# Rounding fp32 weight tiles on ScalarE straight from the load ring, with VectorE subtracting the rounded tile

## The chip, the cores and the metric

The kernel runs on one core of a Trainium2 chip. The metric is the device time of one launch in microseconds (us), the median of three runs. Engines: TensorE (PE) does matrix products, VectorE (DVE) and ScalarE (ACT) elementwise work, GpSimd (POOL) and SyncE (SP) start transfers.

## The reference

Two layers of an encoder trunk on 512 tokens of width 1024, in fp32. Each layer mixes tokens with 16 heads of three kinds (dilated windows, latent attention, two-dimensional neighbourhood), adds the result, and then mixes channels: layer 0 with a dense SwiGLU, layer 1 with a top-2-of-8 expert SwiGLU. The change touches only the dense one:

```python
def swiglu(h, w1, w3, w2):
    return (jax.nn.silu(h @ w1) * (h @ w3)) @ w2
# h: 512 x 1024 (RMS-normed rows), w1, w3: 1024 x 2816, w2: 2816 x 1024
```

## The kernel before

One program, with a hand-written instruction stream for each engine, in program order; engines meet only through semaphores. The dense channel mixer works in two parts each of an fp32 value, kept in the type fp32r: a high part with the low 12 mantissa bits gone, and a low part, the value minus the high part. A product is then three products: low times high, high times low, high times high.

**Gate/up stage** (line 790): 44 jobs. Job j = 2f is the gate, j = 2f + 1 the up projection of feature tile f (0 to 21, 128 features each). A job is 24 matmuls of 128x512: 8 slices of the model width, 3 products each. It takes weight tile w(j), 128x1024, in three buffers of two parts each (`w5`, WS = 3), and the activations x(0) to x(3) (`xh3` high, `xl3` low). The result goes through SiLU (ScalarE, line 1128) and a product (VectorE, line 1460) to the hidden tile h(f), 128x512.

**w2 stage** (line 801): two passes, i = 0 and 1, over output columns 0 to 511 and 512 to 1023. Step f of a pass takes h(f) and weight tile v(i * 22 + f), 128x512, in three buffers of two parts (`v_parts`, VS = 3), for 4 row tiles with 3 products each: 12 matmuls. The last three f of the second pass are done together once the last tile has its parts.

**Who makes the parts.** `low_part(kind, j)` is a piece of VectorE's stream and `high_part(kind, j)` one of ScalarE's. Both follow one list, SPLITS: w0, w1, x0, w2, x1, x2, x3, w3 to w43, h0, v0, v1, then h1, v2, h2, v3, ... h21, v22, then v23 to v43. In `low_part` VectorE masks the value's bits into one of two scratch tiles `high` (line 1346) and subtracts the scratch tile from the value into the low part (line 1353). In `high_part` ScalarE casts the scratch tile into the high part (line 1057). For x and h tiles the high part lies where the value was, so ScalarE also waits for the subtract (line 1051). A part's buffer must be free first (`parts_free`, waited for by the cast and by the subtract, after the mask). TensorE waits for both parts (`parts_made`). Two semaphores are kept in the order of the list, `low_made` and `high_made`; a third, `masked`, counts masks.

**Around the entry.** In layer 0, for each row tile t from 0 to 3, VectorE's order is: add the attention output to x (line 1318), low part of w(t) for t < 3, reciprocal and scaled row (lines 1201 and 1213), then, for row tile t - 1, copy of its transposed half (line 1188) and low part of x(t-1). ScalarE's is: square sum and root of t (lines 985 and 992), high part of w(t), then copy and high part of x(t-1). TensorE runs the output projection of t and transposes the rows of t - 1.

**The ring.** Weights come through `weight_ring`, two halves. An entry is two loads of 1 MB (w1 and w3, four w tiles) or one of 2.8 MB (eleven v tiles). SyncE issues the load of an entry when the low part of the last tile in the entry two before is made (line 461). Nothing in TensorE's or SyncE's stream is changed.

Of the kernel before, what the change touches and what calls it, by code (L numbers as in the profile page):

```python
# [25 lines left out]
ALU = mybir.AluOpType  # L26
# [3 lines left out]
P = 128  # L30
SEQ, D, LAYERS = 512, 1024, 2
# [41 lines left out]
FT = DFF // P  # L73
# [14 lines left out]
WS = 3  # L88
VS = 3
# [65 lines left out]
def split_order():  # L155


    order = [("w", 0), ("w", 1), ("x", 0), ("w", 2), ("x", 1), ("x", 2), ("x", 3)]
    order += [("w", j) for j in range(WS, 2 * FT)] + [("h", 0), ("v", 0), ("v", 1)]
    for f in range(1, FT):  # L160
        order += [("h", f), ("v", f + 1)]
    return order + [("v", n) for n in range(FT + 1, 2 * FT)]


SPLITS = split_order()


def split_of(kind, j):
    return SPLITS.index((kind, j))


class Jobs:
# [27 lines left out]
def trunk(nc, a):  # L200
# [3 lines left out]
    with ctx:  # L204
        def sb(name, cols, dt=F32, rows=P):
            return ctx.enter_context(nc.sbuf_tensor(name, [rows, cols], dt))

        def sem(name):
            return ctx.enter_context(nc.semaphore(name))
# [3 lines left out]
        x = sb("x_rows", NT * D)  # L213
# [64 lines left out]
        xh3, xl3 = (v[:, :].rearrange("p (k s) -> p k s", k=ND) for v in (x_high, x_low))  # L278
# [3 lines left out]
        hh3 = h_high[:, :].rearrange("p (f s) -> p f s", f=FT)  # L282
# [3 lines left out]
        v_parts = [w_parts[:, o:o + 2 * SEQ].rearrange("p (j c) -> p j c", j=2) for o in (4 * D, 5 * D, 3 * D)]  # L286
        w5 = w_parts[:, :].rearrange("p (b j k c) -> p b j k c", b=WS, j=2, k=ND)
        at = (FT + 22) * SEQ
        high = A0[:, at:at + 2 * D].rearrange("p (b k c) -> p b k c", b=2, k=ND)
# [61 lines left out]
        loaded = [sem("ring_loaded_0"), sem("ring_loaded_1")]  # L351
# [20 lines left out]
        masked, low_made, high_made = sem("bits_masked"), sem("low_parts_made"), sem("high_parts_made")  # L372
# [23 lines left out]
        for l in range(LAYERS):  # L396
# [10 lines left out]
            if l == 0:  # L407
                w1, w3, w2 = a["w1"][0], a["w3"][0], a["w2"][0]
# [9 lines left out]
        n_of = {e[0]: n for n, e in enumerate(entries)}  # L418
        loads_to = [0, 0]
        full_at = []  # L420
# [4 lines left out]
        def wview(key, i=0):  # L425
            n = n_of[key]
            o, k, c, _ = entries[n][1][i]
            s = (n % 2) * RING + o
            return ring[:, s:s + k * c].rearrange("p (k c) -> p k c", k=k)
# [6 lines left out]
        NG = 7  # L436

        block = ctx.enter_context(nc.Block())

        def parts_free(engine, kind, j):  # L440

            if kind == "w" and j >= WS:
                engine.wait_ge(filled, J.filled(0, "gu"[(j - WS) % 2], (j - WS) // 2))
            elif kind == "v" and j < VS:
                engine.wait_ge(filled, J.filled(0, "u", FT - 2 if j < 2 else FT - 1))
            elif kind == "v" and j - VS == FT - 1:
                engine.wait_ge(filled, J.filled(0, "d", 0, NT - 1))
            elif kind == "v":
                engine.wait_ge(w2_used, j - VS + 1 - (j - VS >= FT))

        @block.sync
        def _(sp):
# [4 lines left out]
            for n, (key, loads, last) in enumerate(entries):  # L457
                if n >= 2:
                    last_use = entries[n - 2][2]
                    if last_use[0] == "split":  # L460
                        sp.wait_ge(low_made, split_of(*last_use[1:]) + 1)
                    else:
                        sp.wait_ge(filled, J.filled(*last_use))
                for (o, k, c, src) in loads:
                    s = (n % 2) * RING + o
                    sp.dma_start(ring[:, s:s + k * c].rearrange("p (k c) -> p k c", k=k), src)\
                        .then_inc(loaded[n % 2], 16)
                if n == 0:
                    for t in range(2, NT):
                        sp.dma_start(x3[:, t, :], a["x"][0, t * P:(t + 1) * P, :]).then_inc(x_in[t], 16)  # L470
                    sp.dma_start(tab[:, T_COS:], a["tables"][:, T_COS:]).then_inc(tab_in, 16)
# [131 lines left out]
        def _(pe):  # L603
# [75 lines left out]
            for l in range(LAYERS):  # L679
# [104 lines left out]
                if l == 0:  # L784
                    for j in range(2 * FT):
                        b = take(l, "gu"[j % 2], j // 2)
                        parts_made(max(split_of("w", j), split_of("x", NT - 1)))
                        for k in range(ND):
                            for w, xx in ((1, xh3), (0, xl3), (0, xh3)):
                                last = nc.tensor.matmul(b, w5[:, j % WS, w, k, :], xx[:, k, :],  # L790
                                                        start=(k == 0 and w == 1), stop=(k == ND - 1 and xx is xh3 and w == 0))
                        last.then_inc(filled, 1)
# [169 lines left out]
        def _(act):  # L962
# [76 lines left out]
            def second_norm_turned(l, t):  # L1039
                copy_out(split((l, "h2", t, 0)), (l, "h2", t, 0))  # L1040
                if l == 0:
                    high_part("x", t)

            def high_part(kind, j):

                if (kind, j) not in SPLITS:
                    return
                n = split_of(kind, j)
                act.wait_ge(masked, n + 1)
                if kind in "xh":  # L1050
                    act.wait_ge(low_made, n + 1)
                else:
                    parts_free(act, kind, j)
                dst = {"x": lambda: xh3[:, :, j * P:(j + 1) * P], "w": lambda: w5[:, j % WS, 0, :, :],
                       "h": lambda: hh3[:, j, :], "v": lambda: v_parts[j % VS][:, 0, :]}[kind]()
                src = high[:, n % 2] if kind in "xw" else high[:, n % 2].rearrange("p k c -> p (k c)")[:, 0:SEQ]
                nc.scalar.copy(dst, src).then_inc(high_made, 1)  # L1057

            def expo(l, g):
# [11 lines left out]
            for l in range(LAYERS):  # L1071
# [39 lines left out]
                for t in range(NT):  # L1111
                    act.wait_ge(emptied["D"], J.emptied(l, "op", t, 1))
                    x_root(t, A0[:, NT * D:NT * D + D] if l == 0 else yT[:, ND // 2:, :].rearrange("p k s -> p (k s)"))
                    if l == 0 and t < WS:
                        high_part("w", t)
                    if t:
                        second_norm_turned(l, t - 1)
# [56 lines left out]
        def _(dve):  # L1174
# [145 lines left out]
            def low_part(kind, j):  # L1320

                if (kind, j) not in SPLITS:
                    return
                n = split_of(kind, j)
                f = j // 2
                if kind == "x":
                    dve.wait_ge(emptied["A"], J.emptied(0, "h2", j, 0))
                    dve.wait_ge(emptied["D"], J.emptied(0, "h2", j, 1))
                    src, dst = hT3[:, :, j * P:(j + 1) * P], xl3[:, :, j * P:(j + 1) * P]
                elif kind == "h":  # L1330
                    dve.wait_ge(emptied["D"], J.emptied(0, "u", j))
                    src, dst = hid[:, j, :], hl3[j]
                else:
                    if kind == "w":
                        e, v = n_of[(0, "f", f // 2)], wview((0, "f", f // 2), j % 2)
                        src, dst = v[:, :, (f % 2) * P:(f % 2) * P + P], w5[:, j % WS, 1, :, :]
                    else:
                        i, k = divmod(j, FT)
                        c, k = divmod(k, FT // 2)
                        e, src, dst = n_of[(0, "w2", i, c)], wview((0, "w2", i, c))[:, k, :], v_parts[j % VS][:, 1, :]  # L1340
                    dve.wait_ge(loaded[e % 2], full_at[e])
                top_part = high[:, n % 2] if kind in "xw" else high[:, n % 2].rearrange("p k c -> p (k c)")[:, 0:SEQ]
                if n >= 2:
                    dve.wait_ge(high_made, n - 1)
                    dve.wait_ge(low_made, n - 1)
                nc.vector.tensor_scalar(top_part.bitcast(I32), src.bitcast(I32), HIGH, None, ALU.bitwise_and)\  # L1346
                    .then_inc(masked, 1)
                dve.wait_ge(masked, n + 1)
                if kind == "h" and j:
                    dve.wait_ge(filled, J.filled(0, "u", FT - 1))  # L1350
                else:
                    parts_free(dve, kind, j)
                nc.vector.tensor_tensor(dst, src, top_part, ALU.subtract).then_inc(low_made, 1)

            def attention_added(t):
                add_to_x(l, ("op", t, 1), t, 1)
                if l == 0 and t < WS:
                    low_part("w", t)
# [259 lines left out]
```

## Time and profile before

| | |
|---|---|
| median of 3 runs | 2644.17 us (2642.98 to 2645.36) |
| the profiled execution's own time | 2649.0 us |
| its span, first to last instruction | 2647.1 us |
| granted TensorE clock, mean | 0.970 |
| busy: TensorE, VectorE, ScalarE | 93%, 24%, 19% of the span |
| gate/up stage (line 790) | from 425.26 us |
| w2 stage (line 801) | from 671.87 us |

The busy shares are means over the whole kernel; what a change in one stage does is read from that stage. Of a wait that TensorE has, the row says in brackets how long it was idle and who released it. Matmuls overlap in the records: the distance of two starts, not a duration, is what one costs.

### The profile page before, as it was taken

Reading aid. Unit: us, or ns where it says so; the run is one execution under the profiler, and the core shown is the slowest. Engines: PE = TensorE matmul, PEld = TensorE weight load, DVE = VectorE, ACT = ScalarE, POOL = GpSimd, SP = SyncE. Lnnn points to the kernel's source line nnn. Section 1 sums busy time; section 2 is a strip of 40 time slices with the busy share of each in tenths; the row PEclk is TensorE's granted clock in tenths of the full one; section 3 lists DMA queues with packets and bytes.
Section 4 is the critical chain, followed back from the end, with each engine's and each line's share of the span. In section 5 each row is a group of like instructions: output and inputs, shape, how many; then the busy total and the mean of one; then the engine's idle time right before and its main releaser. Section 6 shows DMA issues by size and latency. Waiting matters only on the chain.

```text
span 2647.1 us, 38548 instructions
## 1 busy us (share of the span) xinstructions
PE 2472.9 (93%) x16160; PEld 2162.3 (82%) x16161; DVE 646.9 (24%) x1382; ACT 507.8 (19%) x1032; POOL 115.9 (4%) x100
## 2 busy tenths in 40 slices
PE   8989998999999899997998999999989999999994
PEld 5658656888886568646998999999989999999994
DVE  2146435333742345522000000010000010101003
ACT  1135323222421235411010001001010010100102
POOL 2011000000001020101000000000000000000001
PEclk9999999999999899998999999999999999999997
DMA  8201164223230200144875665776767767788783
GB/s 251 80 13 35 46 222 123 92 92 105 73 118 28 79 32 15 47 167 150 307 295 207 245 230 222 275 261 262 287 255 259 281 252 295 290 309 298 276 302 112
DMA packets 203139, 482.34 MB, mean 182 GB/s; under 512 B 4833, under 2 KB 31600, under 8 KB 202592
## 3 DMA queue, kind: packets, MB, share of 16 engines
q1 hardware_dynamic: 192208, 429.36, 44.2%
q0 software_dynamic: 8304, 40.82, 4.9%
q10 hardware_dynamic: 2448, 9.44, 0.9%
q8 instruction: 154, 2.52, 0.4%
q14 instruction: 25, 0.20, 0.0%
HBM read 459.93 MB, written 35.39 MB: 187 GB/s over the span
## 4 chain that ended last, share of the span: by engine, by line
PE 77%; issue 3%; DVE 2%; ACT 1%; DMA 0%; POOL 0%; DVEq 0%; ACTq 0%; POOLq 0%
PE ps L891 33%; PE ps L906 16%; PE ps L790 9%; PE ps L632 6%; PE ps L801 4%; PE ps L640 3%; PE ps L746 2%; PE ps L625 1%; PE ps L875 1%; PE ps L847 1%; PE ps L859 1%; DVE k_low L1267 0%; ACT qk_high L1026 0%; DVE x_rows L1560 0%; PE ps L726 0%
## 5 line engine op out<-in xcount | busy, mean ns | idle before, releaser
L891 PE MATMUL ps<-hT,attention_arena 128*128 128x128 f32 (+4 forms) x4096 | 530.2, 288 | 43.7 <-issue 43.7
L891 PEld LDWEIGHTS ps<-hT,attention_arena 128*128 128x128 f32 x4096 | 515.3, 195 | 45.5 <-issue 45.5
L1549 DVE TENSOR_TENSOR attention_arena<-ps,attention_arena 128x256 f32<-128x256 f32 x224 | 95.2, 425 | 1238.1 <-ACT attention_arena L1162 1238.1
L891 PE MATMUL ps<-hT,weight_ring 128*128 128x128 f32 (+4 forms) x3072 | 388.6, 283 | 0.0
L891 PEld LDWEIGHTS ps<-hT,weight_ring 128*128 128x128 f32 x3072 | 376.8, 191 | 0.0
L1162 ACT ACTIVATE attention_arena<-ps 128x256 f32<-128x256 f32 x224 | 85.9, 383 | 1128.7 <-PE ps L891 1128.6
L906 PE MATMUL ps<-attention_arena 128*128 128x128 f32 (+4 forms) x2048 | 266.0, 283 | 0.0
L632 PE MATMUL ps<-weight_ring,hT 128*128 128x384 f32 (+3 forms) x768 | 257.6, 496 | 3.3 <-DVE hT L1188 1.7
L906 PEld LDWEIGHTS ps<-attention_arena 128*128 128x128 f32 x2048 | 254.1, 191 | 0.0
L632 PEld LDWEIGHTS ps<-weight_ring,hT 128*128 128x128 f32 x768 | 146.4, 192 | 105.9 <-issue 61.5
L790 PE MATMUL ps<-x_high,w_parts 128*128 128x512 f32 x704 | 223.0, 398 | 5.6 <-ACT x_high L1057 5.6
L906 PE MATMUL ps<-attention_arena,weight_ring 128*128 128x128 f32 (+4 forms) x1536 | 199.5, 283 | 0.0
L906 PEld LDWEIGHTS ps<-attention_arena,weight_ring 128*128 128x128 f32 x1536 | 190.5, 191 | 0.0
L625 PE MATMUL ps<-tables,attention_arena 128*128 128x128 f32 (+1 forms) x840 | 131.1, 288 | 42.3 <-DVE attention_arena L1213 15.6
L625 PEld LDWEIGHTS ps<-tables,attention_arena 128*128 128x128 f32 (+1 forms) x840 | 107.9, 148 | 72.1 <-issue 29.5
L790 PEld LDWEIGHTS ps<-x_high,w_parts 128*128 128x128 f32 x704 | 132.7, 188 | 36.7 <-issue 5.9
L746 PE MATMUL ps<-attention_arena 128*128 128x128 f32 (+1 forms) x1024 | 140.8, 282 | 2.9 <-ACT attention_arena L1100 2.1
L640 PE MATMUL ps<-hT,weight_ring 128*128 128x512 f32 x320 | 141.2, 595 | 0.0
L790 PE MATMUL ps<-x_low,w_parts 128*128 128x512 f32 x352 | 137.8, 392 | 0.0
L746 PEld LDWEIGHTS ps<-attention_arena 128*128 128x128 f32 x1024 | 128.7, 197 | 7.4 <-ACT attention_arena L1100 3.6
L1057 ACT CAST w_parts<-attention_arena 128x1024 fp32r<-128x1024 f32 (+1 forms) x88 | 73.7, 837 | 226.3 <-DVE attention_arena L1346 107.9
L640 PEld LDWEIGHTS ps<-hT,weight_ring 128*128 128x128 f32 x320 | 60.0, 192 | 69.0 <-issue 68.4
(185 smaller groups left out, 1811.5 us busy)
## 6 DMA issues: line engine op xcount, KB each, us to landing
attention_arena<-in_e_w_dram SPq DMA_DIRECT2D x96, 2048.0 KB, 12.3
weight_ring<-in_e_w_dram SPq DMA_DIRECT2D x72, 2048.0 KB, 12.2
weight_ring<-in_w_dram SPq DMA_DIRECT2D x22, 1024.0 KB, 7.3
weight_ring<-in_w_dram SPq DMA_DIRECT2D x4, 2816.0 KB, 10.0
results_by_slot<-attention_arena ACTq DMA_DIRECT2D x9, 1024.0 KB, 9.8
weight_ring<-in_w_o_dram SPq DMA_DIRECT2D x4, 2048.0 KB, 7.9
attention_arena<-rows_by_slot POOLq DMA_DIRECT2D x8, 1024.0 KB, 11.4
weight_ring<-in_w_in_dram SPq DMA_DIRECT2D x2, 3072.0 KB, 10.6
```

The source lines that it names most:

```text
L625: last = nc.tensor.transpose(b[0:w, i * P:(i + 1) * P], s, ident)
L632: last = nc.tensor.matmul(b[:, 0:n], lhsT[:, k, t * P:(t + 1) * P], w[:, k, c0:c0 + n], start=(k == 0), stop=(k == kt - 1))
L640: last = nc.tensor.matmul(b[:, :], w[:, k, c0:c0 + P], hT3[:, k, :], start=(k == 0), stop=(k == ND - 1))
L746: last = nc.tensor.matmul(ob[:, t * P:t * P + v.shape[1]], pt[:, g % 2, k * P:(k + 1) * P], v, start=(k == 0), stop=(k == NT - 1))
L790: last = nc.tensor.matmul(b, w5[:, j % WS, w, k, :], xx[:, k, :], start=(k == 0 and w == 1), stop=(k == ND - 1 and xx is xh3 and w == 0))
L801: last = nc.tensor.matmul(banks[t], h[:, t * P:(t + 1) * P], v[:, j, :], start=(f == 0 and n == 0), stop=(f == FT - 1 and n == 2))
L847: last = nc.tensor.matmul(ps[:, 6 + i % 2, k * UNIT:(k + 1) * UNIT], h4[:, t, (2 * i + k) * P:(2 * i + k + 1) * P], hot[:, t, :], start=(t ...
L891: last = nc.tensor.matmul(ps[:, f % 2, m * UNIT:m * UNIT + n], w[:, k, i * P:(i + 1) * P], XT[:, k, 0:n], start=(k == 0), stop=(k == ND - 1))
L906: last = nc.tensor.matmul(ps[:, 2 + d // 2, at:at + n], w[:, i, d * P:(d + 1) * P], eh[:, f % EHS, 0:n], start=(f == 0 and d % 2 == 0), st ...
L1057: nc.scalar.copy(dst, src).then_inc(high_made, 1)
L1162: nc.scalar.activation(esil[:, f % 2, :], ps[:, f % 2, 0:UNIT], ACT.Silu).then_inc(e_silu, 1)
L1549: tt(eh[:, f % EHS, :], ps[:, f % 2, UNIT:2 * UNIT], esil[:, f % 2, :], ALU.mult).then_inc(gu_free, 1)
```

## The change

Weight tiles (kinds w and v) are no longer masked. ScalarE waits for the load of the ring entry and for the buffer, and casts the tile from the ring to fp32r, which rounds it; VectorE waits for this cast and subtracts the high part from the tile. For x and h tiles mask, subtract and cast stay as they were; their scratch tile is now chosen by their own count, IN_PLACE, and its reuse waits for the cast of the tile two before in that count.

```diff
+IN_PLACE = [n for n, (kind, j) in enumerate(SPLITS) if kind in "xh"]
...
+        def raw_part(kind, j):
+
+            if kind == "w":
+                f = j // 2
+                return n_of[(0, "f", f // 2)], wview((0, "f", f // 2), j % 2)[:, :, (f % 2) * P:(f % 2) * P + P]
+            i, k = divmod(j, FT)
+            c, k = divmod(k, FT // 2)
+            return n_of[(0, "w2", i, c)], wview((0, "w2", i, c))[:, k, :]
...
                 n = split_of(kind, j)
-                act.wait_ge(masked, n + 1)
                 if kind in "xh":
+                    m = IN_PLACE.index(n)
+                    act.wait_ge(masked, m + 1)
                     act.wait_ge(low_made, n + 1)
+                    dst = xh3[:, :, j * P:(j + 1) * P] if kind == "x" else hh3[:, j, :]
+                    src = high[:, m % 2] if kind == "x" else high[:, m % 2].rearrange("p k c -> p (k c)")[:, 0:SEQ]
                 else:
+                    e, src = raw_part(kind, j)
+                    dst = w5[:, j % WS, 0, :, :] if kind == "w" else v_parts[j % VS][:, 0, :]
+                    act.wait_ge(loaded[e % 2], full_at[e])
                     parts_free(act, kind, j)
...
                 nc.scalar.copy(dst, src).then_inc(high_made, 1)
...
                 n = split_of(kind, j)
-                f = j // 2
+                if kind in "wv":
+                    _, src = raw_part(kind, j)
+                    dst = w5[:, j % WS, 1, :, :] if kind == "w" else v_parts[j % VS][:, 1, :]
+                    top_part = w5[:, j % WS, 0, :, :] if kind == "w" else v_parts[j % VS][:, 0, :]
+                    dve.wait_ge(high_made, n + 1)
+                    nc.vector.tensor_tensor(dst, src, top_part, ALU.subtract).then_inc(low_made, 1)
+                    return
...
-                if n >= 2:
-                    dve.wait_ge(high_made, n - 1)
-                    dve.wait_ge(low_made, n - 1)
+                m = IN_PLACE.index(n)
+                top_part = high[:, m % 2] if kind == "x" else high[:, m % 2].rearrange("p k c -> p (k c)")[:, 0:SEQ]
+                if m >= 2:
+                    dve.wait_ge(high_made, IN_PLACE[m - 2] + 1)
                 nc.vector.tensor_scalar(top_part.bitcast(I32), src.bitcast(I32), HIGH, None, ALU.bitwise_and)\
                     .then_inc(masked, 1)
-                dve.wait_ge(masked, n + 1)
+                dve.wait_ge(masked, m + 1)
```

## Rows read from the trace of the kernel before

**Rows 1.** Busy time by stage: us, then busy us (instructions) of each engine, granted clock, DMA share.

```profile
core 0: us, PE busy (x) PEld busy (x) DVE busy (x) ACT busy (x) POOL busy (x), PEclk, DMA share, GB/s
425.00:672.00 247.00, 246.74 (x1057) 199.39 (x1058) 91.90 (x108) 57.37 (x68) 3.04 (x6) 0.99 0.34 108
672.00:733.00 61.00, 61.00 (x268) 49.78 (x267) 47.22 (x91) 26.38 (x43) 0.00 (x0) 1.00 0.24 86
733.00:794.00 61.00, 60.14 (x263) 49.00 (x262) 24.54 (x48) 16.70 (x28) 0.00 (x0) 1.00 0.27 95
```

**Rows 2.** Line 1346 (mask), weight tiles: count, ns min/median/max, first and last start, shapes.

```profile
L1346 DVE TENSOR_SCALAR attention_arena<-weight_ring x88: 417/552/694, 393.2 to 782.9; 128x1024 int32<-128x1024 int32 x44, 128x512 int32<-128x512 int32 x44
```

**Rows 3.** Timeline, the entry: start us, us, engine, line, what [idle before, releaser].

```profile
399.85 1.23 DVE L1353 TENSOR_TENSOR w_parts<-weight_ring,attention_arena 128x1024 fp32r<-128x1024 f32 x1
...
400.64 1.03 ACT L1057 CAST w_parts<-attention_arena 128x1024 fp32r<-128x1024 f32 x1
...
403.89 1.23 DVE L1353 TENSOR_TENSOR x_low<-hT,attention_arena 128x1024 fp32r<-128x1024 f32 x1
...
406.27 0.69 DVE L1318 TENSOR_TENSOR x_rows<-ps,x_rows 128x512 f32<-128x512 f32 x1 [1.15 <-PE ps L632]
...
407.00 1.06 ACT L985 ACTIVATE attention_arena<-x_rows 128x1024 f32<-128x1024 f32 x1 [0.74 <-DVE x_rows L1318]
...
407.60 1.23 DVE L1353 TENSOR_TENSOR w_parts<-weight_ring,attention_arena 128x1024 fp32r<-128x1024 f32 x1
...
408.38 1.03 ACT L1057 CAST w_parts<-attention_arena 128x1024 fp32r<-128x1024 f32 x1
...
411.63 1.23 DVE L1353 TENSOR_TENSOR x_low<-hT,attention_arena 128x1024 fp32r<-128x1024 f32 x1
...
412.95 1.05 ACT L1057 CAST x_high<-attention_arena 128x1024 fp32r<-128x1024 f32 x1 [3.06 <-DVE x_low L1353]
...
414.01 0.69 DVE L1318 TENSOR_TENSOR x_rows<-ps,x_rows 128x512 f32<-128x512 f32 x1 [1.15 <-PE ps L632]
...
414.74 1.06 ACT L985 ACTIVATE attention_arena<-x_rows 128x1024 f32<-128x1024 f32 x1 [0.74 <-DVE x_rows L1318]
...
415.92 0.29 ACT L992 ACTIVATE small<-small,tables 128x1 f32<-128x1 f32 x1
...
416.25 0.16 DVE L1201 RECIPROCAL small<-small 128x1 f32<-128x1 f32 x1 [1.54 <-ACT small L992]
```

**Rows 4.** Timeline of ScalarE and of VectorE, an attention preparation at 211 us.

```profile
211.11 0.58 ACT L1017 CAST qk_high<-ps 96x512 fp32r<-96x512 f32 x1
...
211.80 0.69 DVE L1254 TENSOR_TENSOR q_low<-ps,qk_high 96x512 fp32r<-96x512 f32 x1 [0.41 <-ACT qk_high L1017]
```

**Rows 5.** Timelines of VectorE, ScalarE and TensorE, first pass over w2.

```profile
672.68 0.42 DVE L1346 TENSOR_SCALAR attention_arena<-attention_arena 128x512 int32<-128x512 int32 x1
673.13 0.69 DVE L1353 TENSOR_TENSOR x_low<-attention_arena 128x512 fp32r<-128x512 f32 x1
673.74 0.42 DVE L1346 TENSOR_SCALAR attention_arena<-weight_ring 128x512 int32<-128x512 int32 x1
...
673.91 0.62 ACT L1057 CAST h_high<-attention_arena 128x512 fp32r<-128x512 f32 x1 [6.82 <-DVE x_low L1353]
674.43 0.62 ACT L1057 CAST w_parts<-attention_arena 128x512 fp32r<-128x512 f32 x1
...
674.67 0.47 PE L801 MATMUL ps<-w_parts,x_low 128*128 128x512 f32 x1
...
732.48 0.39 PE L801 MATMUL ps<-w_parts,h_low 128*128 128x512 f32 x1
```

**Rows 6.** Timeline of TensorE, the first matmuls of the gate/up stage.

```profile
425.26 0.77 PE L790 MATMUL ps<-x_high,w_parts 128*128 128x512 f32 x1 [5.56 <-ACT x_high L1057]
...
428.27 0.39 PE L790 MATMUL ps<-x_low,w_parts 128*128 128x512 f32 x1
```

**Rows 7.** Timelines of VectorE and TensorE, the last tile of w2.

```profile
785.03 0.69 DVE L1353 TENSOR_TENSOR w_parts<-weight_ring,attention_arena 128x512 fp32r<-128x512 f32 x1 [1.69 <-PE ps L801]
...
785.78 0.49 PE L801 MATMUL ps<-w_parts 128*128 128x512 f32 x1 [0.86 <-DVE w_parts L1353]
```

More of the change, by code:

```diff
@@ L1048, in high_part @@
                 n = split_of(kind, j)
-                act.wait_ge(masked, n + 1)
                 if kind in "xh":
+                    m = IN_PLACE.index(n)
+                    act.wait_ge(masked, m + 1)
                     act.wait_ge(low_made, n + 1)
-                else:
+                    dst = xh3[:, :, j * P:(j + 1) * P] if kind == "x" else hh3[:, j, :]
+                    src = high[:, m % 2] if kind == "x" else high[:, m % 2].rearrange("p k c -> p (k c)")[:, 0:SEQ]
+                else:
+                    e, src = raw_part(kind, j)
+                    dst = w5[:, j % WS, 0, :, :] if kind == "w" else v_parts[j % VS][:, 0, :]
+                    act.wait_ge(loaded[e % 2], full_at[e])
                     parts_free(act, kind, j)
-                dst = {"x": lambda: xh3[:, :, j * P:(j + 1) * P], "w": lambda: w5[:, j % WS, 0, :, :],
-                       "h": lambda: hh3[:, j, :], "v": lambda: v_parts[j % VS][:, 0, :]}[kind]()
-                src = high[:, n % 2] if kind in "xw" else high[:, n % 2].rearrange("p k c -> p (k c)")[:, 0:SEQ]
                 nc.scalar.copy(dst, src).then_inc(high_made, 1)
@@ L1329, in low_part @@
                     src, dst = hT3[:, :, j * P:(j + 1) * P], xl3[:, :, j * P:(j + 1) * P]
-                elif kind == "h":
+                else:
                     dve.wait_ge(emptied["D"], J.emptied(0, "u", j))
                     src, dst = hid[:, j, :], hl3[j]
[L1333 to L1342, printed above, removed]
-                if n >= 2:
-                    dve.wait_ge(high_made, n - 1)
-                    dve.wait_ge(low_made, n - 1)
+                m = IN_PLACE.index(n)
+                top_part = high[:, m % 2] if kind == "x" else high[:, m % 2].rearrange("p k c -> p (k c)")[:, 0:SEQ]
+                if m >= 2:
+                    dve.wait_ge(high_made, IN_PLACE[m - 2] + 1)
                 nc.vector.tensor_scalar(top_part.bitcast(I32), src.bitcast(I32), HIGH, None, ALU.bitwise_and)\
                     .then_inc(masked, 1)
-                dve.wait_ge(masked, n + 1)
+                dve.wait_ge(masked, m + 1)
                 if kind == "h" and j:
```

## Prediction

> **What bounds the kernel now.** I read three views in order. The table by stage comes first: in the dense channel mixer (425 to 794 us) TensorE is busy 246.74 of 247, 61.00 of 61 and 60.14 of 61 us, at a granted clock of 0.99 to 1.00, while VectorE is busy 91.9, 47.2 and 24.5 us and ScalarE less [rows 1]. So work taken off VectorE is worth nothing here by itself; what counts is when the parts of a tile are ready. Second, the instructions of the mask line: 88 of the 114 masks are on weight tiles, 44 of 1024 columns (0.69 us) and 44 of 512 (0.42 us), 48.8 us of VectorE in all [rows 2]. Third, the timeline of VectorE and ScalarE at the three places where TensorE does wait, or nearly does, for a part: the entry (399 to 425 us), the steps f = 1 to 21 of the first pass over w2 (674 to 733 us) and the last tile of w2 (785 us). All three are weighed below.
>
> **What the change does to the order.** Before, a weight tile cost VectorE mask then subtract, and ScalarE's cast ran beside the subtract. After, ScalarE casts the tile itself and VectorE's subtract waits for that cast. The mask goes (−0.69 or −0.42 us of VectorE), but cast and subtract, which overlapped, now stand one behind the other. On VectorE the waiting subtract holds up whatever is queued behind it: at the entry the reciprocal and normed row of the same t, in the loop over w2 the mask of the next hidden tile. No DMA is added or moved past another in any queue. SP's load into a half of the ring waits for the subtract of the last tile that lay there; the other half then holds four jobs of work (22 us, below), and a load that is asked for 1 to 6 us later is late by that against TensorE too, whose own steps slip with it: nobody waits.
>
> Where the change costs nothing: in the gate/up stage (44 tiles, 41 of them there) a tile is split when its buffer is released and is read two jobs later. A job is 24 matmuls, 247 us over 44 jobs, 5.6 us [rows 1]; cast plus subtract is 1.03 + 1.23 = 2.3 us [rows 3]. Cover is 11 us, so nothing is gained by the mask that goes nor lost by the order. The same holds for the second pass over w2: 0.62 + 0.69 = 1.3 us against two steps of 2.75 us (below).
>
> **The handoff cast to subtract** is not in the old dense code, but the attention preparation does just this: a cast to fp32r from 211.11 for 0.58 us, and a subtract that reads it, from 211.80, so 0.11 us later; it lasts 0.69 us, as long as the subtract with a masked operand [rows 4, 5]. The nearest other case is a root and the reciprocal that waits for it: ends 416.21, starts 416.25, 0.04 us [rows 3]. Bounds 0.04 and 0.11; I take 0.06: nearer to the reciprocal, because the new subtract, like it, has one wait in front of it, where the one at 211 us waits for a bank of TensorE too.
>
> **Term 1, the entry.** The order on VectorE is: add(t), split of w(t), reciprocal and row(t), copy and split of x(t−1). On ScalarE: square and root(t), cast w(t), copy and cast x(t−1) [rows 3].
> - t = 1: cast w1 starts 400.64, lasts 1.03, handoff 0.06: subtract at 401.73 instead of 399.85, +1.88. That also moves the subtract of x0 from 403.89 to 405.77.
> - An instruction begins a little before the one ahead of it ends: 0.08 us on VectorE (673.13 + 0.69 against 673.74), 0.10 on ScalarE (673.91 + 0.62 against 674.43) [rows 5]. So VectorE is free for add(2) 1.23 − 0.08 = 1.15 us after that subtract's start, at 406.92, where TensorE let it go at 406.27: +0.65. The cast of x0 starts 1.32 us after the subtract of x0 (the distance that 411.63 and 412.95 show for x1), at 407.09; ScalarE is free 1.05 − 0.10 later, at 408.04. So square(2) starts at 408.04 instead of 407.00, +1.04: slack of the old order is used up.
> - t = 2: cast w2 408.38 + 1.04 = 409.42, ends 410.45, subtract at 410.51 instead of 407.60, +2.91. The subtract of x1 goes from 411.63 to 414.54, its cast from 412.95 to 415.86.
> - t = 3: add(3) at 414.54 + 1.15 = 415.69 instead of 414.01; square(3) after the cast of x1, at 415.86 + 0.95 = 416.81 instead of 414.74, **+2.1 us**. From here to the first dense matmul at 425.26 everything is a chain without slack (root, row, turn, copy, split x2, copy, split x3; TensorE waits 5.56 us for the last cast) [rows 6], so 2.1 us stays. Bounds: 0, if the shorter split of w hid it all, which the order excludes, and with 0.11 twice 2.2; the low bound with 0.04 is 2.05.
>
> **Term 2, the first pass over w2.** The splits run h1, v2, h2, v3, ... and each queue is in order. Start to start in the old trace [rows 5]: mask h to subtract h 0.45 (672.68, 673.13); subtract h to cast h 0.78 (673.91), since the cast of a hidden tile overwrites its source and waits; cast h to cast v 0.52 (674.43). New: cast v lasts 0.62, handoff 0.06, subtract v; then 0.61 from a subtract's start to the next mask's (673.13, 673.74). This is a ring, as VectorE waits for cast v and ScalarE for subtract h: 0.45 + 0.78 + 0.52 + 0.62 + 0.06 + 0.61 = 3.04 us for each f. In the old order VectorE's own four instructions bounded the loop at 2 × (0.45 + 0.61) = 2.12 us, shorter than TensorE's step. TensorE's step: f = 1 starts at 674.67 and the second pass at 732.48 [rows 5], 21 steps of 2.75 us. The lead is gone already at f = 1: its cast ends at 674.53, 0.14 us before the start. So every step after it is late by 0.29 us more: 20 × (3.04 − 2.75) = 5.8 us, and about 0.1 us for an exposed weight load at the last wait (at 785.78 the first matmul lasts 0.49 against 0.39 [rows 5, 7]): **+5.9 us**. The buffers don't slow the ring, since with a late TensorE v(f+1) has had its buffer free for a step. Bounds: handoff 0.04 gives 3.02 and 5.5, 0.11 gives 3.09 and 6.9.
>
> The loop puts 20 new gaps of some 0.3 us into a stretch without any. After the 5.56 us idle at the entry 7 matmuls take from 425.26 to 428.27, 0.43 us each, which is the 1.2 GHz level [rows 6]; but the 0.86 us wait at 785 left the granted clock of 733 to 794 us at 1.00 [rows 1, 7], and a new gap is a third of it. I take no fall of the clock; it is a rival. The Trainium skill (TensorE: Matmul & The Clock Gate, Part 1: The HAM clock gate) says that the array's clock is gated down to half when TensorE was too little busy of late, which speaks against a change that thins out a full stretch. By that rule, did it bite here, the sum would be that of the rival "the clock falls" below; by the row it is the sum below.
>
> **Term 3, the last tile.** v43's buffer is free when step f = 18 of the second pass ends. Old: subtract at 785.03, for 0.69, matmul at 785.78. New: the cast starts where the subtract did, lasts 0.62, handoff 0.06, subtract at 785.71: **+0.7 us** [rows 7].
>
> **Sum.** 2.1 + 5.9 + 0.7 = 8.7 us. Behind 794 us nothing of the change runs, and the later stages start from the dense result, so the delay goes through to the end. The profiled execution took 2649.0 us with a span of 2647.1; it would take 2657.7, span 2655.8. The median of the runs was 2644.17, 4.8 us under it; with the same sum 2652.9 us. (0.2%, about what a measurement here can tell, is 5.3 us.)
>
> **Rivals.**
> - *The ring is no ring.* If ScalarE or VectorE got ahead (v cast under the subtract of h, say), the loop would stay at TensorE's 2.75 us; then only 2.1 + 0.7: 2647.0 us. For it: the margin is only 0.29 us of 3.04. Against: the program order of both queues. Deciding point: a ring under 2.75.
> - *A dearer ring.* ScalarE now reads a strided slice of the ring, and VectorE reads an fp32r operand beside an SBUF one; no row has just these. The sequence at 211 us says 0.69 us for the subtract. Were cast or handoff 0.2 us longer, the loop would cost 20 × 0.2 = 4.0 more, entry and end 0.6 more: 2657.5 us.
> - *Not slower: the masks take memory time from TensorE.* In gate/up 1056 matmuls fill 246.6 us (247 us less the 0.3 before the first), 0.2335 each; between 672 and 733 the records give 61.00/268 = 0.2276 [rows 1]. Were the masks the difference, 1056 × 5.9 ns = 6.2 us would come back and 2.5 us stay: 2646.7 us, no change that a measurement tells. Against: gate/up has less VectorE work per us (91.9 of 247) than the stage behind it (47.2 of 61), and is the slower [rows 1]. It decides from 3 ns a matmul (3.4 us back, 5.3 left); above 8 ns the kernel would be faster.
> - *The clock falls in the loop.* At 0.43 us a step is 5.16 us: 20 × (5.16 − 3.04) = 42 us more, 2695 us. The wait of 0.86 us that cost no clock speaks against. (The page named under term 2 has the rule by which this could come.)
> - *The change does nothing:* excluded, since the removed masks and the new wait are certain instructions; what can fail is only that they reach TensorE (first rival).
>
> **How the numbers follow.** Forecast 0.66, own range 2651 to 2655; no ring 0.13; dearer ring 0.11; masks steal 0.06; clock 0.02; faster through something I don't see 0.02. Range 2646.5 to 2657: it takes in forecast and "no ring", and leaves out the upper half of the dearer ring, the clock, and what is faster. Faster: 0.03 (the unseen one, a part of the fourth). Slower: forecast nearly whole (0.61), dearer ring and clock, 0.74. Within 0.2%: 0.23.
>
> **What the profile after would show.** Right: mask rows only on x and hidden tiles (26), the subtract of weight tiles each behind its ScalarE cast; first dense matmul at about 427.4; between 676 and 740 us casts of h_high every 3.04 us, and TensorE idle before about 20 matmuls with the h_high cast as releaser, some 0.2 us each; the second pass begun near 740.5; a wait of 1.5 us at the last tile; granted clock 1.00 throughout. Wrong: cast distance still 2.77; or matmul spacing below 0.2334 us in gate/up; or a first dense matmul before 426.

## The result, and the profile after

| | before | changed |
|---|---|---|
| median, us | 2650.34 (9 runs) | 2660.71 (9 runs) |
| lowest to highest | 2642.98 to 2650.90 | 2652.84 to 2661.51 |
| ratio | | 1.0041, 95% interval 1.0029 to 1.0053 |
| the profiled execution: own time, span | 2649.0, 2647.1 | 2660.71, 2658.7 |

The change makes the kernel slower, by 10.4 us in the medians (7.7 to 14.0 by the interval), where 8.7 was forecast. The time itself lies outside the stated range: the nine runs of the kernel before have a median 6.2 us above that of the three which the sum was put on.

The page of the changed kernel, busy time of each engine. VectorE is 41.8 us less busy than before, and the kernel is slower.

```profile
span 2658.7 us, 38285 instructions
...
PE 2482.0 (93%) x16160; PEld 2163.9 (81%) x16161; DVE 605.1 (23%) x1294; ACT 505.8 (19%) x1032; POOL 116.3 (4%) x100
```

Busy time by stage of the changed kernel, for gate/up, first and second pass over w2 [rows 1]:

```profile
429.00:676.00 247.00, 246.99 (x1055) 199.53 (x1056) 67.06 (x66) 57.02 (x67) 2.79 (x6) 0.99 0.33 108
676.00:742.00 66.00, 65.65 (x265) 47.92 (x265) 38.30 (x67) 24.48 (x43) 0.00 (x0) 1.00 0.17 61
742.00:804.40 62.40, 60.91 (x266) 49.63 (x265) 18.85 (x30) 16.63 (x28) 0.00 (x0) 1.00 0.32 113
```

Gate/up is as long as it was, although VectorE works 67 us in it and not 92. The first pass is longer, and TensorE looks nearly as busy in it as ever (65.65 of 66): the recorded durations of matmuls overlap and so cover a gap of 0.2 us. The gaps show in the starts.

Timeline of the changed kernel, the entry (rows of TensorE, VectorE and ScalarE) [rows 3, 6]:

```profile
400.06 1.04 PE L637 MATMUL ps<-tables,attention_arena 128*128 128x128 f32 x8
...
402.37 1.03 ACT L1072 CAST w_parts<-weight_ring 128x1024 fp32r<-128x1024 f32 x1
...
403.43 1.23 DVE L1345 TENSOR_TENSOR w_parts<-weight_ring,w_parts 128x1024 fp32r<-128x1024 f32 x1 [2.48 <-ACT w_parts L1072]
...
411.12 1.03 ACT L1072 CAST w_parts<-weight_ring 128x1024 fp32r<-128x1024 f32 x1
...
412.19 1.23 DVE L1345 TENSOR_TENSOR w_parts<-weight_ring,w_parts 128x1024 fp32r<-128x1024 f32 x1 [2.88 <-ACT w_parts L1072]
...
418.50 1.05 ACT L997 ACTIVATE attention_arena<-x_rows 128x1024 f32<-128x1024 f32 x1
...
429.01 0.77 PE L802 MATMUL ps<-x_high,w_parts 128*128 128x512 f32 x1 [5.50 <-ACT x_high L1072]
```

The first row is the transposes of row tile 0. The same row of the kernel before, with those at which its first pass over w2 begins and its second ends:

```profile
398.33 1.04 PE L625 MATMUL ps<-tables,attention_arena 128*128 128x128 f32 x8
...
671.87 0.39 PE L801 MATMUL ps<-w_parts,h_low 128*128 128x512 f32 x1
...
794.07 1.03 PE L625 MATMUL ps<-tables,attention_arena 128*128 128x128 f32 x8
```

So the transposes stood at 398.33. All of this stretch is 1.73 us late already when it begins, and that comes from ahead of the changed code. Set against its own beginning, the first dense matmul comes at 28.95 us (429.01 − 400.06), before at 26.93 (425.26 − 398.33). VectorE now waits 2.48 and 2.88 us for the casts of w1 and w2. The square sum of row tile 3 starts at 418.50, 2.03 us later than before on the same clock (414.74 + 1.73).

Timelines of the changed kernel, first pass over w2 [rows 5]:

```profile
677.54 0.69 DVE L1365 TENSOR_TENSOR x_low<-attention_arena 128x512 fp32r<-128x512 f32 x1
679.49 0.69 DVE L1345 TENSOR_TENSOR w_parts<-weight_ring,w_parts 128x512 fp32r<-128x512 f32 x1 [1.26 <-ACT w_parts L1072]
680.10 0.42 DVE L1358 TENSOR_SCALAR attention_arena<-attention_arena 128x512 int32<-128x512 int32 x1
680.56 0.69 DVE L1365 TENSOR_TENSOR x_low<-attention_arena 128x512 fp32r<-128x512 f32 x1
...
678.32 0.62 ACT L1072 CAST h_high<-attention_arena 128x512 fp32r<-128x512 f32 x1 [6.82 <-DVE x_low L1365]
678.85 0.62 ACT L1072 CAST w_parts<-weight_ring 128x512 fp32r<-128x512 f32 x1
681.34 0.62 ACT L1072 CAST h_high<-attention_arena 128x512 fp32r<-128x512 f32 x1 [1.87 <-DVE x_low L1365]
...
676.28 0.40 PE L813 MATMUL ps<-w_parts,h_low 128*128 128x512 f32 x1
...
679.08 0.47 PE L813 MATMUL ps<-w_parts,x_low 128*128 128x512 f32 x1
...
682.10 0.47 PE L813 MATMUL ps<-w_parts,x_low 128*128 128x512 f32 x1
...
742.24 0.39 PE L813 MATMUL ps<-w_parts,h_low 128*128 128x512 f32 x1
```

The ring in these rows: subtract h 677.54, cast h 678.32, cast v 678.85 (ends 679.47), subtract v 679.49, mask h 680.10, subtract h 680.56. One round is 3.02 us. Both helpers are idle in it, VectorE 1.26 and ScalarE 1.87 us, each waiting for the other, and TensorE for both (679.08 to 682.10). The rows of line 813 in the changed kernel name this idle time:

```profile
its engine sat idle before it (us, times) until:
  issue: 8.6, 21
  DVE w_parts L1345: 3.4, 2
```

Twenty-one gaps have no releaser: the profile gives them to "issue", on the weight load, not to the cast of h_high as the prediction had it. The first of them (0.30 us, at 679) stands in the kernel before too (0.28); the other twenty are the change's. What they wait for has to be read from the equal distances: the casts of h_high are 3.02 us apart over the whole pass, and so are TensorE's steps.

Timelines of the changed kernel, the last tile [rows 7]:

```profile
794.77 0.62 ACT L1072 CAST w_parts<-weight_ring 128x512 fp32r<-128x512 f32 x1 [2.10 <-PE ps L813]
...
795.42 0.69 DVE L1345 TENSOR_TENSOR w_parts<-weight_ring,w_parts 128x512 fp32r<-128x512 f32 x1 [2.02 <-ACT w_parts L1072]
...
796.17 0.50 PE L813 MATMUL ps<-w_parts 128*128 128x512 f32 x1 [1.49 <-DVE w_parts L1345]
```

1.49 us idle where it was 0.86.

### The profile page after: what moved, and what is told of

It is laid out like the page before. It is cut to its first block, busy times and chain, and to the rows that moved or that the text cites. A ratio compares the mean times of both kernels' runs of the same rounds, so it can differ in the third digit from the quotient of the medians.

```text
span 2658.7 us, 38285 instructions
## 1 busy us (share of the span) xinstructions
PE 2482.0 (93%) x16160; PEld 2163.9 (81%) x16161; DVE 605.1 (23%) x1294; ACT 505.8 (19%) x1032; POOL 116.3 (4%) x100
## 4 chain that ended last, share of the span: by engine, by line
PE 77%; issue 3%; DVE 2%; ACT 1%; DMA 0%; POOL 0%; DVEq 0%; ACTq 0%; POOLq 0%
PE ps L903 33%; PE ps L918 16%; PE ps L802 9%; PE ps L644 6%; PE ps L813 5%; PE ps L652 3%; PE ps L758 2%; PE ps L637 1%; PE ps L887 1%; PE ps L859 1%; PE ps L871 1%; DVE k_low L1282 0%; ACT qk_high L1038 0%; DVE x_rows L1572 0%; PE ps L738 0%
## 5 line engine op out<-in xcount | busy, mean ns | idle before, releaser
L1345 DVE TENSOR_TENSOR w_parts<-weight_ring,w_parts 128x1024 fp32r<-128x1024 f32 (+1 forms) x88 | 84.2, 958 | 180.5 <-ACT w_parts L1072 180.5
```

## The experiments

The theory (A): the loss is the serial order of cast and subtract at three places, and nothing else of the change costs or saves. Its rivals (B and C in the expectations): the masks disturb TensorE; the direct rounding or the fp32r operand is dear by itself; the change slows something outside the dense stage.

The main evidence is one table of stages, a profile of each kernel. A stage runs between the starts of TensorE instructions: entry, from the transposes of row tile 0 (line 625 before, at 398.33) to the first gate/up matmul; then gate/up, the first pass, and the second pass with its last tile up to the first transposes of layer 1 (at 794.07 before). Outside is the span less these four. us:

| kernel | entry | gate/up | pass 1 | pass 2 | sum | outside | ratio to before, 95% |
|---|---|---|---|---|---|---|---|
| before | 26.9 | 246.6 | 60.6 | 61.6 | 395.7 | 2251.4 | |
| before_again | 26.9 | 247.6 | 60.6 | 61.6 | 396.7 | 2246.5 | one run |
| changed | 29.0 | 247.3 | 66.0 | 62.2 | 404.4 | 2254.3 | 1.0041 (1.0029 to 1.0053) |
| after_again | 29.0 | 246.7 | 65.9 | 62.2 | 403.8 | 2248.0 | 1.0029 (1.0020 to 1.0038) |
| after_third | 29.0 | 247.3 | 66.0 | 62.2 | 404.4 | 2255.1 | one run |
| only_w | 29.0 | 246.6 | 60.6 | 61.6 | 397.8 | 2250.8 | 1.0007 (0.9998 to 1.0015) |
| only_v | 26.9 | 247.6 | 66.0 | 62.2 | 402.7 | 2254.3 | 1.0025 (1.0015 to 1.0034) |
| order_alone | 29.1 | 247.2 | 67.9 | 62.3 | 406.5 | 2254.1 | 1.0052 (1.0039 to 1.0065) |
| order_one_wait | 28.9 | 246.7 | 66.0 | 62.2 | 403.8 | 2247.8 | 1.0044 (1.0031 to 1.0057) |
| mask_first | 29.0 | 247.3 | 60.6 | 62.2 | 399.1 | 2248.1 | 1.0013 (1.0004 to 1.0022) |
| cast_early | 26.9 | 246.6 | 66.0 | 62.2 | 401.7 | 2249.7 | 1.0031 (1.0022 to 1.0040) |
| all_mended | 26.9 | 246.6 | 60.6 | 60.9 | 395.0 | 2250.9 | 1.0002 (0.9993 to 1.0011) |

Entry, pass 1 and pass 2 repeat to 0.1 us from launch to launch. Outside doesn't: 2246.5 to 2255.1. That is why the three stages, and not the whole time, decide below.

**after_again: the changed kernel once more.**

> The changed kernel once more, beside the kernel before on the same chip. Theory A (the serial order of cast and subtract makes the loss at three places; what is left of the difference is the granted clock elsewhere): from the first transposes of the second norm to the first transposes of layer 1 it takes 404.4 us again, against 395.7 before, so 8.7 us more, and the rest of the span differs from the first profile by some us in either direction with the granted clock. Theory B (the change costs time outside the dense stage too): the stretches outside are 3 us longer than before again.

2655.67 us against 2648.03: +7.6. The dense stage takes 403.8 us, as expected by A within the scatter of gate/up; outside it is 3.4 us shorter than in the unchanged kernel's first profile, and 1.5 longer than in its second, where B asked for 3 us longer.

**only_w and only_v: each half of the change.**

```diff
+RAW = "w"
-IN_PLACE = [n for n, (kind, j) in enumerate(SPLITS) if kind in "xh"]
+IN_PLACE = [n for n, (kind, j) in enumerate(SPLITS) if kind not in RAW]
...
-                if kind in "wv":
+                if kind in RAW:
...
```

only_v has "v" there. The other kind of weight tile keeps its mask, its scratch tile and the old waits.

> Only the w tiles (gate/up) are rounded straight from the ring, v tiles are masked as before. Theory A: 2.0 us over before, all of it between the second norm and the first dense matmul; h_high casts about 2.75 us apart. Theory C (44 masks of 0.69 us fewer speed gate/up): gate/up shorter by 3 us or more, so at most as slow as before.

> Only the v tiles (w2) are rounded straight from the ring, w tiles are masked as before. Theory A: 6.0 us over before, 5.4 in the first pass over w2 and 0.6 at the last tile; no change at the entry. Rival: the loop is slow only because TensorE comes to it with another lead after the late entry; then under 3 us.

only_w has the changed kernel's entry and the old kernel's two passes; only_v the reverse. The stage sums are 2.1 and 7.0 us over before; without gate/up, 2.1 and 6.0. In only_w gate/up takes 246.6 us with its masks of weight tiles gone, exactly as in the first profile of before: masks don't disturb TensorE there. That the late entry changes the lead at the loop is out too. In time: 2650.18 (+2.2, with an interval that takes in no change) and 2655.41 (+7.4).

**order_alone: the old masks, the new order.**

```diff
                     parts_free(dve, kind, j)
+                if kind in "wv":
+                    dve.wait_ge(high_made, n + 1)
                 nc.vector.tensor_tensor(dst, src, top_part, ALU.subtract).then_inc(low_made, 1)
```

> The kernel before, masks and scratch tile kept, with one wait added: the subtract of a weight tile waits for ScalarE's cast of it. Theory A (order alone): the masks lie in VectorE's waiting time, so it is as slow as the changed kernel, 8 to 9 us over before; casts of hidden tiles 3.02 us apart in the first pass over w2. Theory B (the direct rounding, a strided source or an fp32r operand, costs its own time): less than 4 us over before. Theory C (the masks disturb TensorE): gate/up is at 0.2335 us a matmul here and faster in the changed kernel.

The order alone gives the whole loss, 10.8 us in the stages, so the loss needs neither the rounding from the ring nor the fp32r operand. But it gives more than the whole: 2662.57 us, +14.5, and a round of the ring of 3.12 us (688.96 − 685.84), not 3.02. Timelines of order_alone:

```profile
686.37 0.61 ACT L1057 CAST w_parts<-attention_arena 128x512 fp32r<-128x512 f32 x1
688.96 0.62 ACT L1057 CAST h_high<-attention_arena 128x512 fp32r<-128x512 f32 x1 [1.97 <-DVE x_low L1355]
...
687.11 0.69 DVE L1355 TENSOR_TENSOR w_parts<-weight_ring,attention_arena 128x512 fp32r<-128x512 f32 x1 [1.02 <-ACT w_parts L1057]
```

The cast ends at 686.98 and the subtract starts at 687.11: a handoff of 0.13 us, where the changed kernel has 0.02 by its rounded rows (679.47, 679.49) and 0.03 by the trace's nanoseconds, in each of the 21 rounds. Neither theory expected that. The subtract here has three waits in front of it (mask, buffer, cast), the changed one a single wait.

**order_one_wait: the same with one wait.**

```diff
-                dve.wait_ge(masked, n + 1)
+                dve.wait_ge(high_made if kind in "wv" else masked, n + 1)
                 if kind == "h" and j:
                     dve.wait_ge(filled, J.filled(0, "u", FT - 1))
-                else:
+                elif kind in "xh":
                     parts_free(dve, kind, j)
```

> As the kernel with the order alone (masks kept, subtract behind the cast), but its subtract has one wait in front of it, for the cast; the waits for the mask and for the buffer, which the cast has had already, are dropped. If the 0.13 us between cast and subtract there comes of the three waits in a row, it is 0.02 here, the hidden tiles' casts are 3.02 apart and the first pass takes 65.9 us like the changed kernel, not 67.9. If it comes of the masked operand or the mask ahead, it stays at 67.9.

Timelines of order_one_wait:

```profile
684.34 0.61 ACT L1057 CAST w_parts<-attention_arena 128x512 fp32r<-128x512 f32 x1
686.83 0.62 ACT L1057 CAST h_high<-attention_arena 128x512 fp32r<-128x512 f32 x1 [1.88 <-DVE x_low L1353]
...
684.99 0.69 DVE L1353 TENSOR_TENSOR w_parts<-weight_ring,attention_arena 128x512 fp32r<-128x512 f32 x1 [0.93 <-ACT w_parts L1057]
```

Cast ends 684.95, subtract 684.99: 0.04 us by the rows, 0.03 by the nanoseconds, as in the changed kernel. The round is 3.01 (686.83 from the 683.82 before it), the first pass 66.0 us. So the kernel with all its masks and one wait has the changed kernel's entry and passes to 0.1 us (2657.07 us, +9.0), and the direct rounding costs nothing by itself. The two waits on events long past were worth 20 × 0.1 = 2 us in a ring.

**mask_first: VectorE masks the next hidden tile before it waits.**

```diff
...
                 n = split_of(kind, j)
+                if kind == "v" and 2 <= j <= FT:
+                    low_part("h", j, True)
                 if kind in "wv":
...
```

The call makes the mask of h(j) alone, and low_part of h(j) then leaves it out.

> The changed kernel, with VectorE's mask of the next hidden tile put ahead of the subtract of the weight tile before it, so that the mask lies in the wait for ScalarE's cast. Theory A (a ring through both queues): the ring loses the mask's 0.45 us, 3.02 becomes 2.57, under TensorE's 2.75; the first pass over w2 goes from 65.95 us back to 60.6, entry and last tile stay at 28.9 and 62.2. Rival (TensorE pays for each wait on fresh parts, whatever the ring is): the pass stays above 63 us.

Timeline of VectorE in mask_first:

```profile
683.70 0.68 DVE L1373 TENSOR_TENSOR x_low<-attention_arena 128x512 fp32r<-128x512 f32 x1
684.30 0.42 DVE L1364 TENSOR_SCALAR attention_arena<-attention_arena 128x512 int32<-128x512 int32 x1
685.64 0.69 DVE L1349 TENSOR_TENSOR w_parts<-weight_ring,w_parts 128x512 fp32r<-128x512 f32 x1 [0.93 <-ACT w_parts L1072]
686.25 0.68 DVE L1373 TENSOR_TENSOR x_low<-attention_arena 128x512 fp32r<-128x512 f32 x1
```

The mask lies in the wait, the round is 2.55 us (686.25 − 683.70), under TensorE's 2.75, and the first pass takes 60.6 us, the old time. The same work in the same two queues, one instruction moved: this is the ring shown. In time +3.8 us (2651.89 against 2648.06), where the stages leave 2.0 + 0.6 and gate/up's scatter.

**cast_early: ScalarE casts w1 and w2 before it waits for the row sums.**

```diff
                 for t in range(NT):
+                    if l == 0 and 0 < t < WS:
+                        high_part("w", t)
                     act.wait_ge(emptied["D"], J.emptied(l, "op", t, 1))
                     x_root(t, ...)
-                    if l == 0 and t < WS:
+                    if l == 0 and t == 0:
                         high_part("w", t)
```

> The changed kernel, with ScalarE casting w1 and w2 before it waits for the row sums of their t, not after. Theory A (the entry is late because the subtract of w stands behind square, root and cast): entry back from 28.9 to 27.0 us, everything else as changed. Rival (the clock or the load of the first weights makes the entry late): entry stays at 28.9.

Timeline of VectorE in cast_early:

```profile
399.55 0.69 DVE L1335 TENSOR_TENSOR x_rows<-ps,x_rows 128x512 f32<-128x512 f32 x1 [1.07 <-PE ps L644]
400.15 1.22 DVE L1347 TENSOR_TENSOR w_parts<-weight_ring,w_parts 128x1024 fp32r<-128x1024 f32 x1
...
407.29 0.69 DVE L1335 TENSOR_TENSOR x_rows<-ps,x_rows 128x512 f32<-128x512 f32 x1 [1.36 <-PE ps L644]
408.04 1.23 DVE L1347 TENSOR_TENSOR w_parts<-weight_ring,w_parts 128x1024 fp32r<-128x1024 f32 x1
```

No wait for a cast is left, VectorE is ahead of TensorE again (1.36 us idle before the third add, 1.15 in the old kernel), and the entry is 26.9 us. It is not shorter than the old 26.9, though VectorE does two masks less: VectorE's adds wait for TensorE's projection, so that sets the time. In time it is +8.2 us (2656.25 against 2648.06), where the stages leave 6.0. One of its twelve launches took 5904.76 us; no profile shows why, and the ratio is taken without it.

**all_mended: both mends, and the last three v tiles waited for one by one.**

```diff
-                            parts_made(len(SPLITS) - 1)
                             for t in range(NT):
                                 for f in range(FT - behind, FT):
+                                    if t == 0:
+                                        parts_made(split_of("v", i * FT + f))
                                     last = product(f, t)
```

> The changed kernel with both mends (mask of the next hidden tile first, casts of w1 and w2 early), and TensorE waiting for the parts of each of the last three v tiles before it first reads it, not for all of them at once. Theory A: entry 27.0, first pass 60.6, and the 1.5 us wait at the last tile covered by two products of 0.68 us each, second pass 62.2 minus 1.3 is 60.9; the dense stage takes 395 us against 395.7 before and 404 changed. In the whole time 0 to 1 us under before, which only the stage can show. Rival: a fourth wait appears and it stays 2 us or more over before.

Timeline of TensorE in all_mended, at the last tile:

```profile
788.05 0.61 PE L813 MATMUL ps<-w_parts,h_high 128*128 128x512 f32 x2
788.80 0.50 PE L813 MATMUL ps<-w_parts 128*128 128x512 f32 x1
```

From the last matmul pair to the next, 0.75 us instead of 0.45: of the 1.49 us wait 0.3 is left. The dense stage takes 395.0 us, 0.7 less than in the first profile of before and 1.7 less than in the second. In time it is 2647.88 against 2648.06, the same. It beats the changed kernel clearly and the kernel before by its stages alone. The gain is in pass 2 (60.9 against 61.6) and comes of the last tile's waits. The old kernel could have those without the change; no run tries it.

**before_again and after_third: the time outside.**

> The unchanged kernel, profiled once more. Theory A (what lies outside the dense stage scatters with the granted clock, whatever the kernel): the dense stage takes 395.7 us again (395.5 to 396.5, by how many matmuls of gate/up fall on the low clock), and the time outside, 2251.4 us in the first profile, comes out 1 to 4 us different. Theory B (the change made the outside slower): outside it is 2251.4 within 0.5 us.

> The changed kernel, profiled a third time. Theory A: the dense stage takes 403.8 to 404.5 us, and the time outside lies anywhere between the 2248.0 and 2254.3 us of its first two profiles, or a few us beside. Theory B: outside above 2254 again.

The two profiles of the unchanged kernel differ by 4.9 us outside the dense stage (2251.4, 2246.5), which is more than A's 1 to 4 and rules out B's half a microsecond; the dense stage is a little above A's 396.5. The three of the changed one are 2254.3, 2248.0 and 2255.1. The last is what B said, and A had left room for it, so after_third decides nothing.

The time outside goes with the granted clock (the third column from the right). Over the whole span it is 0.970 and 0.972 in the two profiles of before, and 0.967, 0.972 and 0.968 in the three of the changed kernel: with 0.972 the outside takes 2246.5 and 2248.0 us, with 0.967 and 0.968 2254.3 and 2255.1. The two old profiles differ in it behind the dense stage, from 900 to 1000 us (before, then before_again):

```profile
900.00:1000.00 100.00, 86.58 (x395) 58.85 (x394) 45.04 (x116) 37.15 (x77) 20.30 (x11) 0.90 0.11 38
...
900.00:1000.00 100.00, 85.36 (x421) 58.52 (x420) 48.82 (x127) 39.78 (x84) 21.87 (x13) 0.95 0.11 33
```

From 100 to 200 us, ahead of all changed code, both have 0.95. There the changed kernel differs from itself; busy time in before_again, in the changed kernel's first profile, and in after_again:

```profile
100.00:200.00 100.00, 87.97 (x349) 54.70 (x347) 37.94 (x97) 29.02 (x59) 12.65 (x6) 0.95 0.12 42
```

```profile
100.00:200.00 100.00, 89.15 (x342) 55.86 (x342) 35.88 (x94) 29.15 (x59) 12.65 (x6) 0.91 0.09 32
```

```profile
100.00:200.00 100.00, 88.78 (x351) 55.28 (x349) 36.83 (x95) 29.44 (x60) 12.65 (x6) 0.95 0.12 41
```

So the same kernel has 0.91 or 0.95. Whether casting from the ring draws the 0.91 more often stays open. Of the eight profiles of kernels that do so (changed, after_again, after_third, only_w, only_v, mask_first, cast_early, all_mended) six have it, of the four with every mask in place none: few profiles, but it isn't nothing. And in eight of the nine comparisons the whole time is further above before than entry and the two passes account for, by 0.1 to 4.3 us. What that is, no run shows. Launches of equal granted clock agree with the stages: at 0.972 the changed kernel's five average 2653.3 us and eight of before 2645.6, 7.7 apart.

## Why the prediction was right and where it was wrong

- *Direction, mechanism and places*: right. Three terms were forecast and three were found. Moving one instruction undid each of the first two, and waiting tile by tile hid the third. The dense stage lost 8.7 us in the first pair of profiles (404.4 − 395.7), and the sum was 8.7, but that match is partly luck: the three terms come to 8.0, and 0.7 is scatter of gate/up.
- *Term 1, entry, 2.1*: measured 2.0. The chain by which two small delays exceed VectorE's and then ScalarE's slack went as worked out.
- *Term 2, first pass, 5.9*: measured 5.4 (742.24 − 676.28 against 732.48 − 671.87 is 65.96 − 60.61). Mis-sized by the handoff: 0.06 taken, 0.03 measured, so the ring is 3.02 and not 3.04. The low bound, 0.04 and 5.5 us, was just not low enough. The row at 211 us, 0.11, has two waits in front of its instruction, and order_alone's 0.13 has three: the argument that one wait is cheaper was right in kind.
- *Term 3, last tile, 0.7*: measured 0.6 (1.49 − 0.86).
- *Gate/up, 0*: 0.7 longer in the first pair of profiles, and not by the change: the unchanged kernel has 246.6 and 247.6. Here the low clock holds for more or fewer of the first matmuls.
- *No loss in masks, no fall of the clock in the loop*: right. The rival of the masks was itself mis-sized: 268 counts matmuls that lie partly outside the stretch, and 264 in 60.61 us are 0.2296 us each, 3.9 ns less than in gate/up and not 5.9, so it was worth 4.1 us and not 6.2. The granted clock of the first pass is 1.00 with 21 gaps in it. The Trainium skill (TensorE: Matmul & The Clock Gate, Part 1: The HAM clock gate) has the clock gated down when TensorE is too little busy; no run here thins the loop enough to show that. The entry agrees with it: after 5.5 us idle the first 7 to 10 matmuls take 0.43 us each.
- *The step that failed* is "with the same sum 2652.9 us" and the range around it. The sum was put on the median of three runs, 2644.17, and the range held only the unknown prices of the change, nothing for the base. Nine runs of the same kernel gave 2650.34, 28 in a later comparison 2648.03: the base scatters by 8 us (2642.88 to 2650.91), as much as the whole effect. 2650.34 + 8.7 would have been 2659.0, against 2660.71, and with the 8.0 that the stages show 2658.3: the last 2.4 us lie outside the three places and stay open. The profiled execution's 2649.0, which the prediction set beside the median and then left, lay nearer.
- *"Behind 794 us nothing of the change runs, so the delay goes through"*: it goes through, and the rest of the kernel adds its own scatter, 1.7 us ahead of the entry and 1.2 behind the dense stage in the first pair. These 2.9 us make the span's 11.6 out of 8.7. A second comparison of the same two kernels gave 7.6 us in the medians, so the size of the effect is 7.6 to 10.4 us, with 8.0 shown in the stages (2.0 + 5.4 + 0.6).

## What to carry to other kernels

Taking work off a helper engine that the busiest engine does not wait for gains nothing, and if the work taken off was what let two helpers run side by side, it costs. When two in-order queues hand tiles to each other in both directions, write down one round start to start, in one line of numbers, and compare it with the consumer's step; if it is longer, move an instruction that waits for nobody into the wait. And when the effect is a third of a per cent, measure it between two instructions around the changed stage, where it repeats to 0.1 us, and give the whole time a range at least as wide as the runs of the kernel before scatter.

## What the runs showed of the hardware

- In the first pass VectorE's subtract, behind a single wait, starts 0.03 us after the ScalarE cast that it waits for ends (the changed kernel and order_one_wait); with two more waits in front of it, both on events long past, 0.13 us (order_alone). With all else equal this made the first pass 67.9 and not 66.0 us.
- The fp32r operand and the source in the ring, strided for w tiles, are free: the cast lasts 0.61 to 0.63 us for 512 and 1.03 to 1.06 us for 1024 columns from the ring as from the scratch tile, the subtract 0.69 and 1.23 with either.
- Gaps of 0.2 us every 3 us left TensorE's granted clock at 1.00 in the first pass (676 to 742 us).
- After the 5.5 us idle at the entry, gate/up takes 246.6 to 247.6 us in launches of the same kernel (before and before_again): the step from the 1.2 to the 2.4 GHz level comes at another matmul each time. In the first profile of before 7 matmuls take 0.43 us each, in that of the changed kernel 10 (429.01 to 433.37).
